# A two-layer mixed trunk on one core: turning products over four PSUM banks, partial sums kept in the rows, rope cut in two, weight and token sums placed one by one

## The chip, the cores and the metric

The kernel runs on one core of a Trainium2 chip. The metric is the device time of one launch in microseconds. The engines are named as in the profile: PE (TensorE matmul, with PEld for its weight loads), DVE (VectorE), ACT (ScalarE), POOL (GpSimd) and SP (SyncE, whose queue issues most transfers). All engines take their instructions in order; they meet at semaphores only.

## The reference: what is computed

A trunk of two layers over 512 tokens of width 1024, with 256 context tokens, all in fp32. The first layer (window attention beside a two-way state-space scan) is not touched. The second is a differential attention over the 768 tokens; cut to what matters:

```python
q, k, v, g = split(h @ w_in, 4)              # h: 768 x 1024 (q, g only for the 512 tokens), w_in: 1024 x 4096
q, k = rope(rms_norm(q, q_norm)), rope(rms_norm(k, k_norm))   # per 64-wide half head; context keys have no rope
s = einsum('bqhcd,bkhcd->bchqk', q, k) * 64 ** -0.5           # 8 heads, 2 components c
p = softmax(s)
o = einsum('bhqk,bkhv->bqhv', p[:, 0] - lam * p[:, 1], v)
o = rms_norm(o, head_norm) * (1 - lambda_init)
x = x + gate * ((o * silu(g)) @ w_out)
```

## The kernel before

The program is one list of stages, `STAGES`, written out by hand; every engine walks the same list and does its own part of each stage. The order of the list is therefore the order of work on PE, DVE, ACT and POOL alike. `stages_layer1` (line 265) writes the second layer.

**Products.** `h @ w_in` is done in eight slabs of 512 columns, in the order k1 0, q1 0, v1 0, g1 0, k1 1, q1 1, v1 1, g1 1. Within a slab two token tiles of 128 make a pair (three pairs with the context, two without), and a pair times a slab is done as a 2 x 2 block product with seven multiplications instead of eight, stages `("pr", kind, n, pair, i)` with i from 0 to 6. Each is four matmuls of depth 128 on 256 columns, which the trace shows as eight passes (line 1215). Products 0, 2, 4 and 6 add up in one PSUM bank, 1 and 3 in another (the cross bank), 5 stands alone. ACT copies 0, 1 and 2 out as partial sums and 6 as a final quarter (line 1979); DVE adds 3, 4 and 5 to the partial sums 2, 1 and 0 and so makes the other three quarters (line 1733). A product starts once the one before it in its bank has been copied or added out (`begin`, `unit_done`). Before the change `unit_banks` (line 368) gives products banks 0 and 1 alone, and the partial sums have three places of their own in the weight ring, so ACT waits for the add of the pair before (`PAIR_BEFORE`).

**Sums.** The block product needs sums of token blocks, four for a pair (`("sa", pair, j)`, lines 1753 to 1761), and sums of weight blocks, four for a slab (`("tw", slab, j)`, lines 1771 to 1781). All are DVE's. Products 1 to 4 of a pair wait for token sums 0 to 3; products 1, 2, 4 and 6 for weight sums 0 to 3.

**Rows of k1 and q1.** For each token tile: ACT squares the rows (line 1992), DVE reduces the squares by head (stage `heads`, line 1583), POOL makes the inverse root (lines 2148 and 2149), and DVE ropes the rows and multiplies by the root (stage `rope`; lines 1298, 1307 and 1309 inside `ropes`, and 1593). The first `heads` stage also makes the gain tables of the rope (lines 1314 and 1320) and sets `pads_ready` behind them (line 1573). ACT's copy of the very first product waits for that mark, because the rows of k1 lie over the raw rope table.

**Attention.** 32 steps (8 heads by 4 token tiles). In each: scores (PE, line 1243), their maxima (DVE, 1637), two exponentials (ACT, 2112), their difference (DVE, 1797), transposes of the step before (PE 1256, copied by ACT 2119), products with v (PE 1266), squares (ACT 2126) and the eviction times the gate (DVE 1806). The transposes of a step wait for line 1806 of an earlier one. Every fourth step ends with a head norm (root on POOL, DVE 1814). Stage `otr` transposes a finished head's output; DVE evicts the even heads (1820) and ACT the odd ones (2132). Some three to five products stand in each of the first 16 steps.

The place where such things stand in the list decides what waits for what. The first stages of the layer:

```python
st = [("k1", 0, 4), ("norm", 1, NX - 1), ("k1", 0, 5), ("tw", 0, 0), ("tw", 0, 1)]
st += [("trn", 1, k, 0) for k in range(KD)]
st += [("sa", 0, 0), ("sa", 0, 1), ("heads", "k1", 0, 4), ("sa", 0, 2), ("tw", 0, 2), ("sa", 0, 3),
       ("heads", "k1", 0, 5), ("tw", 0, 3)]
```

`trn` transposes the normed rows on PE; DVE (line 1397) and ACT (line 1900) evict them by turns into hT, which all products read.

## Time and profile before

| | us |
|---|---|
| median of 3 runs (lowest, highest) | 1134.08 (1131.03, 1134.19) |
| the profiled execution, its own time | 1134.98 |
| its span, first to last instruction | 1133.1 |
| PE busy | 1075.9 |
| DVE busy | 653.4 |
| ACT busy | 365.8 |
| POOL busy | 175.6 |

A row of a timeline gives the start and the length of one instruction or of several alike in a row, the engine, the line, the tiles out<-in, and in brackets how long the engine had stood idle before and what released it. The granted clock of PE is given as a share of 2.4 GHz. Durations of matmuls are modelled at their end, so the distance from start to start tells more than one row's length.

### The profile page before, as it was taken

To read this page: it belongs to the slowest core of one execution; us is meant where nothing else is said; L and a number is where in the kernel's file an instruction comes from. 1 tells how busy PE (TensorE), PEld (TensorE's weight loads), DVE (VectorE), ACT (ScalarE), POOL (GpSimd) and SP (SyncE) were. 2 spreads that over 40 slices of the span, in tenths; PEclk is the share of its full clock that TensorE was granted. 3 is DMA by queue.
4 is the path that set the end of the run, shared out by engine and by line. 5 is a ranking of instruction groups with operands and counts; after the bars stand their busy time and mean duration, and the time that the engine had idled before them with its cause. 6 is when DMAs were issued, how large, how long until landed. Compare 5 with 4: busy or idle time off the path is not lost. (4 is left out here: it accounts for less than half of the span.)

```text
span 1133.1 us, 13225 instructions
## 1 busy us (share of the span) xinstructions
PE 1075.9 (95%) x4708; PEld 681.9 (60%) x4708; DVE 653.4 (58%) x1332; ACT 365.8 (32%) x872; POOL 175.6 (15%) x168
## 2 busy tenths in 40 slices
PE   4999999999999999999999987999998989999998
PEld 2665656555454444555544456787887768776663
DVE  0356677596727377776411247834577764577683
ACT  1522212145322344554200121212443333354450
POOL 0111000397623100000000003310022110000000
PEclk9899999999999999999999999999999989999999
DMA  9912440586750110010021030222202030204002
GB/s 353 338 10 79 154 158 6 183 286 215 257 224 31 56 57 1 1 56 1 1 79 51 37 126 0 76 74 75 75 2 74 1 112 1 75 1 149 1 1 75
DMA packets 50982, 100.64 MB, mean 89 GB/s; under 512 B 4388, under 2 KB 6309, under 8 KB 50917
## 3 DMA queue, kind: packets, MB, share of 16 engines
q1 hardware_dynamic: 44997, 88.77, 22.4%
q10 hardware_dynamic: 5664, 10.84, 2.6%
q0 software_dynamic: 256, 0.18, 0.4%
q8 instruction: 39, 0.64, 0.2%
q14 instruction: 26, 0.21, 0.1%
HBM read 93.38 MB, written 6.40 MB: 88 GB/s over the span
## 5 line engine op out<-in xcount | busy, mean ns | idle before, releaser
L928 PE MATMUL ps<-hT,ring 128*128 128x512 f32 (+1 forms) x512 | 169.8, 486 | 1.2 <-ACT pool_mem L1926 0.7
L1215 PE MATMUL ps<-ring,hT 128*128 128x256 f32 x608 | 140.4, 385 | 13.3 <-DVE pool_mem L1733 12.0
L928 PEld LDWEIGHTS ps<-hT,ring 128*128 128x128 f32 x512 | 95.8, 190 | 66.3 <-issue 60.3
L1215 PEld LDWEIGHTS ps<-ring,hT 128*128 128x128 f32 x608 | 114.7, 192 | 32.1 <-issue 15.9
L1215 PE MATMUL ps<-ring,xs_all 128*128 128x256 f32 x432 | 100.4, 389 | 6.6 <-ACT pool_mem L1979 3.0
L1215 PEld LDWEIGHTS ps<-ring,xs_all 128*128 128x128 f32 x432 | 83.4, 195 | 20.5 <-issue 8.8
L2148 POOL TENSOR_SCALAR stat<-stat 128x1 f32<-128x1 f32 (+2 forms) x32 | 9.1, 284 | 545.0 <-ACT pool_mem L1879 209.1
L1116 PE MATMUL ps<-ring,hT 128*128 128x512 f32 x192 | 88.4, 594 | 0.1
L1188 PE MATMUL ps<-ring,hT 128*128 128x512 f32 x192 | 85.8, 592 | 0.0
L1637 DVE TENSOR_REDUCE stat<-ps 128x1 f32<-128x768 f32 x64 | 60.9, 952 | 9.9 <-PE ps L1243 9.8
L1413 DVE SCALAR_TENSOR_TENSOR pool_mem<-ps,halftap,pool_mem 128x254 f32<-128x254 f32 (+3 forms) x96 | 59.1, 616 | 3.4
L2112 ACT ACTIVATE xs_all<-ps,stat 128x768 f32<-128x768 f32 x64 | 57.4, 903 | 11.1 <-DVE stat L1638 10.5
L1188 PEld LDWEIGHTS ps<-ring,hT 128*128 128x128 f32 x192 | 35.5, 190 | 40.2 <-issue 40.2
L928 PE MATMUL ps<-ring,pool_mem 128*128 128x512 f32 x128 | 57.8, 595 | 1.1 <-ACT pool_mem L2132 0.8
L1723 DVE TENSOR_TENSOR pool_mem<-ps,pool_mem 128x512 f32<-128x512 f32 x12 | 8.3, 692 | 84.2 <-PE ps L1188 84.2
L928 PE MATMUL ps<-ring,hT 128*128 128x512 f32 x128 | 56.0, 593 | 0.0
L1266 PEld LDWEIGHTS ps<-y_all,pool_mem 128*128 128x128 f32 x384 | 48.9, 195 | 7.3 <-issue 5.0
L1116 PEld LDWEIGHTS ps<-ring,hT 128*128 128x128 f32 x192 | 33.7, 190 | 30.6 <-issue 30.6
L1266 PE MATMUL ps<-y_all,pool_mem 128*128 128x128 f32 x384 | 48.9, 278 | 0.0
L2052 ACT COPY pool_mem<-ps 128x256 f32<-128x256 f32 (+2 forms) x48 | 26.2, 546 | 59.7 <-PE ps L1157 59.7
L1188 PE MATMUL ps<-ring,pool_mem 128*128 128x512 f32 x96 | 43.8, 593 | 0.0
L1088 PE MATMUL ps<-pool_mem 128*128 128x512 f32 x80 | 40.1, 626 | 2.8 <-DVE stat L1549 2.8
(226 smaller groups left out, 1629.7 us busy)
## 6 DMA issues: line engine op xcount, KB each, us to landing
ring<-in_mod_w_dram SPq DMA_DIRECT2D x10, 2048.0 KB, 8.7
ring<-in_od_w_in_dram SPq DMA_DIRECT2D x8, 2048.0 KB, 8.2
ring<-in_ev_w_in_dram SPq DMA_DIRECT2D x7, 2048.0 KB, 9.5
pool_mem<-la_rows_dram SPq DMA_DIRECT2D x24, 512.0 KB, 7.6
ring<-in_ev_w_out_dram SPq DMA_DIRECT2D x4, 1536.0 KB, 6.6
ring<-in_od_w_out_dram SPq DMA_DIRECT2D x2, 2048.0 KB, 10.0
ring<-in_mod_w_dram ACTq DMA_DIRECT2D x1, 2048.0 KB, 9.2
xs_all<-in_x_dram SPq DMA_DIRECT2D x4, 512.0 KB, 12.9
```

The source lines that it names most:

```text
L928: mm = pe.matmul(bank[:, 0:width], lhs_of(k), rhs_of(k), start=(k == 0), stop=(k == count - 1))
L1088: pe.matmul(ps[:, (2, 4)[n % 2], :], lhs, rhs, start=True, stop=True).then_inc(st_ready, 1)
L1116: mm = pe.matmul(bank, hT[:, k, t * P:(t + 1) * P], w[:, k, :], start=(k == 0), stop=(k == KD - 1))
L1188: mm = pe.matmul(bank, src[:, t * P:(t + 1) * P], slab_ap(("out0", n, k // 6))[:, k % 6, :], start=(k == 0), stop=(k == KM - 1))
L1215: mm = pe.matmul(bank[:, 0:NSPLIT], left[:, k, :], right[:, k, :], start=(k == 0 and i in (0, 1, 5)), stop=(k == KSPLIT - 1), skip_group_c ...
L1266: mm = pe.matmul(bank[:, 2 * P:3 * P], probT1[:, j, :], v1v[:, j, h * P:(h + 1) * P], start=(j == 0), stop=(j == NT - 1))
L1413: ins_ = V.scalar_tensor_tensor(out=dst[:, lo:hi], in0=src[:, lo + j - 2:hi + j - 2], scalar=tap(j), in1=dst[:, lo:hi], op0=ALU.mult, op1= ...
L1637: link(V.tensor_reduce(rmax[:, r:r + 1], pair(n)[:, 0:TOK], AXX, ALU.max))
L1723: V.tensor_tensor(tmp, bank_of(stage), gate, ALU.mult).then_inc(done_sem(stage), 1)
L2052: A.copy(probT[:, 0:nb, i, :], pt_bank[:, 0:nb * P].rearrange("p (b t) -> p b t", b=nb)).then_inc(pt_done, 1)
L2112: A.activation(prob1[:, c, :], pair(n)[:, 0:TOK], ACT.Exp, bias=nmax[:, r:r + 1], scale=SCALE, accum_out=rsum[:, r:r + 1]).then_inc(prob1_ ...
L2148: link(G.tensor_scalar(dst, src, 1.0 / count, EPS, ALU.mult, ALU.add))
```

## The change

- Products whose pair ends ahead of attention take the least recently used of four banks that isn't held (banks 0, 1, 7 and 5 of PSUM); later ones have banks 0 and 1 as before. PE waits once for the last use of bank 5 ahead of the first scores, and once for that of bank 7 ahead of the first transposed probabilities.
- ACT copies a partial sum straight to the rows that it belongs to, and DVE adds onto it in place. The three places in the ring and ACT's wait for the pair before are gone.
- The rope is two stages: part 0 multiplies by cosine and sine, part 1 adds the two and multiplies by the root. Parts are put into the list one behind each product. Where a tile's `heads` stage would have ended a step of attention, it now follows the first product of the next one.
- The weight sums of the next slab come behind products 0, 3 and 5 of the last pair and product 1 of the next slab (before: 0, 2, 4, 6). In the first slab the sums of the second and third pair come one behind each product; the sums of the first pair and all weight sums of the first slab stand ahead of product 0, and the `heads` stages of the context tiles behind products 0 and 1.
- ACT evicts all eight transposed outputs.

```diff
 def slab_products(s):
+    sums = {}
+    if s + 1 < len(IN_SLABS):
+        sums = {0: ("tw", s + 1, 0), 3: ("tw", s + 1, 1), 5: ("tw", s + 1, 2)}
...
-            if last and s + 1 < len(IN_SLABS) and i % 2 == 0:
-                piece.append(("tw", s + 1, i // 2))
+            if last and i in sums:
+                piece.append(sums[i])
+            if p == 0 and i == 1 and s >= 1:
+                piece.append(("tw", s, 3))
...
+def new_heads(piece):
+    return [u[1:] for u in piece if u[0] == "post" and u[1] != "g1"]
...
-    st = [("k1", 0, 4), ("norm", 1, NX - 1), ("k1", 0, 5), ("tw", 0, 0), ("tw", 0, 1)]
+    st = [("k1", 0, 4), ("norm", 1, NX - 1), ("k1", 0, 5), ("tw", 0, 0)]
     st += [("trn", 1, k, 0) for k in range(KD)]
-    st += [("sa", 0, 0), ("sa", 0, 1), ("heads", "k1", 0, 4), ("sa", 0, 2), ("tw", 0, 2), ("sa", 0, 3),
-           ("heads", "k1", 0, 5), ("tw", 0, 3)]
-    st += [("sa", 1, j) for j in range(4)]
+    st += [("sa", 0, 0), ("sa", 0, 1), ("tw", 0, 1), ("sa", 0, 2), ("sa", 0, 3), ("tw", 0, 2), ("tw", 0, 3)]
+    extra = {(0, 0): ("heads", "k1", 0, 4), (0, 1): ("heads", "k1", 0, 5), (0, 2): ("rope", 1, "k1", 0, 4),
+             (0, 3): ("sa", 1, 0), (0, 4): ("sa", 1, 1), (0, 5): ("rope", 1, "k1", 0, 5), (0, 6): ("sa", 1, 2),
+             (0, 7): ("sa", 1, 3), (1, 0): ("sa", 2, 0), (1, 2): ("sa", 2, 1), (1, 4): ("sa", 2, 2), (1, 6): ("sa", 2, 3),
+             (2, 10): ("hk", 0, 1), (2, 13): ("hk", 0, 0), (2, 17): ("hq", 0)}
...
             st += piece
-            st += squares
-            squares = head_stages(piece, "heads")
-            if ropes and j % 7 in (0, 2):
+            st += [("heads",) + u for u in squares]
+            if ropes:
                 st.append(ropes.pop(0))
-            ropes += head_stages(piece, "rope")
+            ropes += [("rope", part) + u for u in fresh for part in range(2)]
+            fresh, squares = squares, new_heads(piece)
...
-            if j == min(1, len(now) - 1) and waiting:
-                st.append(waiting[0])
-            if j == 3 and two:
-                st.append(waiting[1])
-        st += squares
-        squares = []
+            if ropes and (j >= 1 or len(now) == 1):
+                st.append(ropes.pop(0))
+            ropes += [("rope", part) + u for u in fresh for part in range(u[2] >= NX, 2)]
+            fresh, squares = squares, new_heads(piece)
...
-BANKS = (0, 1, 7)
+BANKS = (0, 1, 7, 5)
...
-                bank[m] = min((b for b in range(2) if b not in held), key=lambda b: last[b])
+                free = [b for b in ((0, 1, 2, 3) if STAGES.index(u[:4] + (6,)) < attention else (0, 1)) if b not in held]
+                bank[m] = min(free, key=lambda b: last[b])
...
                         pe.wait_ge(prob_ready, len(SCORE))
+                        pe.wait_ge(unit_done[3], UNIT_BANK.count(3))
...
                         pe.wait_ge(pt_done, len(SCORE))
+                        pe.wait_ge(unit_done[2], UNIT_TURN[UNIT[PV1S[0]]])
...
-                        V.tensor_tensor(odd_rows(sub, n, t)[:, half * NSPLIT:(half + 1) * NSPLIT],
-                                        bank_of(stage)[:, 0:NSPLIT], part_sum[5 - i], ALU.add
+                        rows = product_rows(*a)
+                        V.tensor_tensor(rows, bank_of(stage)[:, 0:NSPLIT], rows, ALU.add
...
-                            dst = part_sum[i]
-                            if (sub, n, p) in PAIR_BEFORE:
-                                wait_done(act, ("pr",) + PAIR_BEFORE[(sub, n, p)] + (5 - i,))
                         if stage == ("pr", "k1", 0, 0, 0):
                             act.wait_ge(pads_ready, 2)
-                        A.copy(dst, bank_of(stage)[:, 0:NSPLIT]).then_inc(done_sem(stage), 1)
+                        A.copy(product_rows(*a), bank_of(stage)[:, 0:NSPLIT]).then_inc(done_sem(stage), 1)
...
-                    if h % 2 == 1:
-                        wait_unit(act, stage)
+                    wait_unit(act, stage)
+                    A.activation(oT[h], bank_of(stage), ACT.Copy, scale=head_gain).then_inc(done_sem(stage), 1)
```

## Rows read from the trace of the kernel before

**Rows 1.** The page's first part: busy us (share of span) and instructions of each engine.

```profile
PE 1075.9 (95%) x4708; PEld 681.9 (60%) x4708; DVE 653.4 (58%) x1332; ACT 365.8 (32%) x872; POOL 175.6 (15%) x168
```

**Rows 2.** Stretches of layer 2: from:to, length, busy PE, PEld, DVE, ACT, POOL, clock, DMA.

```profile
674.00:782.00 108.00, 96.49 (x437) 81.95 (x438) 66.34 (x132) 19.02 (x45) 25.69 (x20) 0.98 0.17 59
...
782.00:1024.00 242.00, 226.63 (x1222) 185.07 (x1223) 154.28 (x305) 95.15 (x218) 26.44 (x28) 0.98 0.12 43
...
680.00:720.00 40.00, 32.41 (x142) 27.44 (x141) 32.02 (x60) 5.87 (x13) 15.22 (x12) 0.96 0.15 53
```

**Rows 3.** Timeline, all engines, 670 to 690: start, length, engine, line, tiles, [idle before].

```profile
670.07 1.23 DVE L1777 TENSOR_TENSOR ring<-ring 128x1024 f32<-128x1024 f32 x1
...
672.16 1.94 PE L997 MATMUL ps<-consts,y_all 128*128 128x128 f32 x16 [1.72 <-DVE hT L1397]
...
675.07 0.69 DVE L1753 TENSOR_TENSOR xs_all<-hT 128x512 f32<-128x512 f32 x1 [0.48 <-ACT hT L1900]
...
675.08 1.97 PE L1215 MATMUL ps<-ring,hT 128*128 128x256 f32 x8 [0.97 <-DVE hT L1397]
...
676.40 0.42 DVE L1314 TENSOR_TENSOR pool_mem<-pool_mem,bc 128x256 f32<-128x256 f32 x1
...
678.27 0.15 DVE L1573 COPY stat<-ones 128x1 f32<-128x1 f32 x1
...
678.51 0.66 ACT L1979 COPY ring<-ps 128x256 f32<-128x256 f32 x2 [3.54 <-DVE stat L1573]
...
679.03 3.69 PE L1215 MATMUL ps<-ring,xs_all 128*128 128x256 f32 x16 [0.26 <-ACT ring L1979]
...
680.18 1.22 DVE L1779 TENSOR_TENSOR ring<-ring 128x1024 f32<-128x1024 f32 x1
...
689.65 6.79 PE L1215 MATMUL ps<-ring,hT 128*128 128x256 f32 x24 [5.20 <-DVE pool_mem L1733]
```

**Rows 4.** The same timeline, on DVE: one product's add, and one rope.

```profile
693.03 0.42 DVE L1733 TENSOR_TENSOR pool_mem<-ps,ring 128x256 f32<-128x256 f32 x1 [3.19 <-PE ps L1215]
...
696.53 0.68 DVE L1298 TENSOR_TENSOR pool_mem<-pool_mem 128x512 f32<-128x512 f32 x1
...
698.06 0.69 DVE L1309 TENSOR_TENSOR pool_mem<-pool_mem 128x512 f32<-128x512 f32 x1
...
698.78 0.69 DVE L1593 TENSOR_TENSOR pool_mem<-pool_mem,dcd 128x512 f32<-128x512 f32 x1
```

**Rows 5.** Timeline of PE alone, 690 to 790.

```profile
696.28 5.34 PE L1215 MATMUL ps<-ring,xs_all 128*128 128x256 f32 x24
...
704.50 5.42 PE L1215 MATMUL ps<-ring,hT 128*128 128x256 f32 x24 [1.15 <-DVE pool_mem L1733]
...
755.26 0.41 PE L945 MATMUL ps<-consts,pool_mem 128*128 128x128 f32 x2 [0.61 <-DVE y_all L1733]
```

**Rows 6.** Timeline, all engines, 842 to 882.

```profile
856.52 1.97 PE L1215 MATMUL ps<-ring,pool_mem 128*128 128x256 f32 x8 [2.22 <-ACT ring L1979]
...
862.10 2.77 PE L1215 MATMUL ps<-ring,hT 128*128 128x256 f32 x8 [1.89 <-DVE pool_mem L1733]
...
867.42 0.69 DVE L1583 TENSOR_REDUCE dcd<-pool_mem 128x8 f32<-128x512 f32 x1 [0.81 <-ACT pool_mem L1992]
...
868.48 0.88 PE L1256 MATMUL ps<-consts,xs_all 128*128 128x128 f32 x6
```

**Rows 7.** Timeline, all engines, 896 to 932.

```profile
906.75 0.69 DVE L1583 TENSOR_REDUCE dcd<-pool_mem 128x8 f32<-128x512 f32 x1 [0.81 <-ACT pool_mem L1992]
...
910.85 0.69 DVE L1814 TENSOR_TENSOR pool_mem<-pool_mem,stat 128x512 f32<-128x512 f32 x1 [3.16 <-POOL stat L2149]
...
915.12 8.39 PE L1215 MATMUL ps<-ring,xs_all 128*128 128x256 f32 x24 [3.03 <-ACT pool_mem L1979]
```

**Rows 8.** Timeline, all engines, 946 to 984.

```profile
976.85 0.80 ACT L2119 COPY pool_mem<-ps 128x768 f32<-128x768 f32 x1 [2.27 <-PE ps L1256]
...
978.60 5.42 PE L1215 MATMUL ps<-ring,xs_all 128*128 128x256 f32 x24 [1.79 <-DVE pool_mem L1820]
```

More of the change, by code:

```diff
@@ L257, in slab_products @@
     return out
-def head_stages(piece, name):
-    return [(name,) + u[1:] for u in piece if u[0] in ("post", "k1") and u[1] != "g1"]
+def new_heads(piece):
+    return [u[1:] for u in piece if u[0] == "post" and u[1] != "g1"]
 def stages_layer1():
-    st = [("k1", 0, 4), ("norm", 1, NX - 1), ("k1", 0, 5), ("tw", 0, 0), ("tw", 0, 1)]
+    st = [("k1", 0, 4), ("norm", 1, NX - 1), ("k1", 0, 5), ("tw", 0, 0)]
     st += [("trn", 1, k, 0) for k in range(KD)]
-    st += [("sa", 0, 0), ("sa", 0, 1), ("heads", "k1", 0, 4), ("sa", 0, 2), ("tw", 0, 2), ("sa", 0, 3),
-           ("heads", "k1", 0, 5), ("tw", 0, 3)]
-    st += [("sa", 1, j) for j in range(4)]
-    turns = {10: ("hk", 0, 1), 13: ("hk", 0, 0), 17: ("hq", 0)}
-    squares, ropes = [], [("rope", "k1", 0, 4), ("rope", "k1", 0, 5)]
+    st += [("sa", 0, 0), ("sa", 0, 1), ("tw", 0, 1), ("sa", 0, 2), ("sa", 0, 3), ("tw", 0, 2), ("tw", 0, 3)]
+    extra = {(0, 0): ("heads", "k1", 0, 4), (0, 1): ("heads", "k1", 0, 5), (0, 2): ("rope", 1, "k1", 0, 4),
[3 rows of a table added]
+    squares, ropes, fresh = [], [], []
     for s in range(3):
@@ L275, in stages_layer1 @@
             st += piece
-            st += squares
-            squares = head_stages(piece, "heads")
-            if ropes and j % 7 in (0, 2):
+            st += [("heads",) + u for u in squares]
+            if ropes:
                 st.append(ropes.pop(0))
-            ropes += head_stages(piece, "rope")
-            if s == 1 and j in (0, 2, 4, 6):
-                st.append(("sa", 2, j // 2))
-            if s == 2 and j in turns:
-                st.append(turns[j])
-    assert not ropes and not squares
+            ropes += [("rope", part) + u for u in fresh for part in range(2)]
+            fresh, squares = squares, new_heads(piece)
+            if (s, j) in extra:
+                st.append(extra[(s, j)])
+    assert not ropes and not squares and not fresh
     fill = [piece for s in range(3, len(IN_SLABS)) for piece in slab_products(s)]
@@ L307, in stages_layer1 @@
         now = [fill.pop(0) for _ in range(STEP_PRODUCTS[n])] if n < len(STEP_PRODUCTS) else [outs.pop(0)]
-        waiting = ropes
-        two = len(waiting) > 1 and len(now) > 3
-        ropes = waiting[1 + two:]
         for j, piece in enumerate(now):
             st += piece
-            st += squares
-            squares = head_stages(piece, "heads")
-            ropes = ropes + head_stages(piece, "rope")
+            st += [("heads",) + u for u in squares]
             if j == 0:
                 st.append(("comb1", h, t))
-            if j == min(1, len(now) - 1) and waiting:
-                st.append(waiting[0])
-            if j == 3 and two:
-                st.append(waiting[1])
-        st += squares
-        squares = []
+            if ropes and (j >= 1 or len(now) == 1):
+                st.append(ropes.pop(0))
+            ropes += [("rope", part) + u for u in fresh for part in range(u[2] >= NX, 2)]
+            fresh, squares = squares, new_heads(piece)
         if n >= 1:
@@ L330, in stages_layer1 @@
             st.append(("hnorm", n // 4 - 1))
-    assert not fill and not ropes
+    assert not fill and not ropes and not fresh and not squares
     st += [("ptr1",) + work[-1]] + outs.pop(0) + [("pv1",) + work[-1], ("hnorm", C_HEADS - 1)]
@@ L370, in unit_banks @@
     bank, turn = [None] * len(UNITS), [None] * len(UNITS)
-    last, turns, held, sums, cross = [-2, -1, -3], [0, 0, 0], set(), None, None
+    last, turns, held, sums, cross = [-2, -1, -3, -4], [0, 0, 0, 0], set(), None, None
+    attention = STAGES.index(("sc1", 0, 0, 0))
     for n, s in enumerate(STAGES):
@@ L1288, in _, with ropes @@
             V = nc.vector
-            def ropes(src, groups, wtab, wrow, token_tile, ta, tb):
+            def ropes(src, groups, wtab, wrow, token_tile, ta, tb, part=None):
                 v = src.rearrange("p (h d) -> p h d", d=HD)
@@ L1295, in ropes @@
                     link(V.tensor_tensor(a, v, wrow.unsqueeze(1).to_broadcast([P, groups, HD]), ALU.mult))
+                    return
+                if part == 1:
+                    link(V.tensor_tensor(ta[:, 0:groups * HD], ta[:, 0:groups * HD], tb[:, 0:groups * HD], ALU.add))
                     return
```

29 lines of the change are left out of this document (11 added, 18 removed).

## Prediction

> **What bounds the kernel now.** I read the page's busy shares first, then the stretches of the second layer, then PE's waits there in order of time. PE is busy for 1075.9 us of the span [rows 1], and the chain that ends last runs on PE, so only PE's gaps and its slow stretches can be won. The diff touches the second layer from its first product on. There PE stands still for 11.5 of the 108 us up to the first attention score, and for 15.4 of the 242 us in which products and attention are mixed (span less busy time) [rows 2]. The clock matters as well: a stretch of three products takes 5.34 us at full clock [rows 5], 6.79 us after the long gap in the first pair [rows 3] (the granted clock of 680 to 720 is 0.96 of 2.4 GHz on the mean [rows 2], so a part ran at 1.2 GHz) and 8.39 us after a later gap [rows 7]. So a gap can be paid twice, once as idle time and once at the lower of the two clock levels. I price every edit by what PE waited for at that place, and take its clock loss from the row behind the gap.
>
> One product is eight passes; three take 5.34 us with an overlap of 0.15 us, so one is worth about 1.73 us [rows 5].
>
> **The change, part by part.**
>
> *Start of the layer.* Before, the second weight sum (1.23 us) runs on DVE ahead of its evictions of the normed rows, and PE then waits 1.72 us for such an eviction [rows 3]. The change puts that sum behind the evictions. The wait shrinks to about 0.4 us and everything up to the first product comes 1.3 us earlier: product 0 at 673.8 instead of 675.1.
>
> *A new wait, at the third product.* ACT may copy product 0 only when the raw rope table has been read, since the rows of k1 lie over it. Before, DVE made four sums short of that: two token sums, then the gain tables from 676.40, done with the marker at 678.27; ACT copied at 678.51 and PE's third product started at 679.03 with 0.26 us of waiting [rows 3]. In the changed order all four token sums and three weight sums stand on DVE ahead of the gain tables: 4 x 0.7 + 3 x 1.2 = 6.4 us, from 673.8 to 680.2; the tables take 2.0 us (676.40 to the end of the marker at 678.42), so the marker falls at 682.2 and the third product starts 0.6 us later, at 682.8. Products 0 and 1 end at 677.3. That is a gap of 5.5 us on PE, and on ACT the copies of products 0 and 1 queue behind it. The third product adds into the bank of product 0, so four banks don't help.
>
> *The old gap goes.* Before, product 5 waited 5.20 us, to 689.65, because DVE had weight sums, the next pair's token sums and two ropes ahead of one add [rows 3]. Now these sums are spread one behind each add. Products 2, 3 and 4 run behind the new gap; with the slow clock of the old one (6.65 us net for three, from 6.79) product 5 starts at 682.8 + 6.65 = 689.4. The next pair starts two products later, at 692.9; before it was 689.65 + 6.79 - 1.73 = 694.7. Gain 1.8 us. Bounds: 3.2 us if the clock stays up (5.34 instead of 6.79), 0.2 us if it falls as in the 8.39 us row.
>
> *Four banks, and rope in two stages, in the k1 and q1 slabs.* In the three following pairs product 5 waits for the add of product 3, 1.15 to 1.24 us each, three rows of which one stands [rows 5]: with two banks it needs that bank, and DVE does a whole rope first (2.9 us, 696.53 to the end of 698.78 [rows 4]). With four banks product 5 takes another bank, and the waiting one is product 6, which needs the add of product 4. Behind the add of product 3 (0.42 us) DVE has a weight sum (1.2), the first rope stage (1.5 us: 696.53 to 698.06) and then the add of product 4: 3.6 us, against two products, 3.46 us. I leave 0.3 us of waiting in two of the three pairs: gain 3.0 us; between 0 (DVE falls behind, it is busy for 32.02 of 40 us there [rows 2]) and 3.6. The ropes' second stages hold only adds that nobody waits for so soon.
>
> *The three transposes of heads ahead of attention.* Two of them wait 0.61 us for an add (one row stands [rows 5]). In the new turn they fall on banks 0 and 1 when these hold nothing fresh. Gain 1.2 us (0 to 1.2). PE's two added waits at the first scores and the first transposed probabilities stand ahead of everything on PE, but the last products in those banks are four products old; nothing, or at most 0.61 us if the cover is gone.
>
> *Partial sums in the rows.* The same copies and adds, the same sizes; only ACT's wait for the pair before goes, and no PE gap rests on it. Nothing.
>
> *Attention, step with both ropes and a head norm ahead (850 to 868).* PE's gap of 2.22 us comes from ACT copying late behind its exponentials and stays [rows 6]. The 1.89 us at 862.10 goes: the add now comes behind one rope stage. But DVE must still do two weight sums, two ropes, three adds before it evicts the attention output that the next transposes wait for (868.48), and the only thing that leaves the step is one squares reduction with its wait for ACT (0.81 + 0.69 us, of which some is given back in hand-overs): that transpose comes 0.7 us earlier, and the gap moves ahead of it, now some 3 us in one piece. If the clock answers as behind the other gap of this size (3.03 us, then 8.39 instead of 5.34 [rows 7]), up to 3.05 us are lost where before the slow stretch was hidden. I take half, 1.6: a loss of 0.9 us, between a gain of 0.7 and a loss of 2.4.
>
> *Attention, step 896 to 915.* Here the same reduction (0.81 of wait, 0.69 of work) moves across the step's end, and with it POOL's root. In the old order POOL makes that root first and the head norm's root behind it, so DVE stands 3.16 us at 910.85, the scores' maxima and the exponentials come late, ACT copies late, and PE waits 3.03 us at 915.12 and then runs slowly [rows 7]. In the new order the head norm's root is long made. DVE reaches the norm when its step's work is done, 0.8 us before the old reduction's end at 907.4 plus 0.35 us for the eviction, about 907.05; 3.8 us earlier, and the products with it. No gap of that length is left ahead of them, so I also count the clock: 8.39 - 5.34 = 3.05. Gain 6.9 us (3.8 to 6.9).
>
> *Transposed outputs evicted by ACT alone.* At 978.60 PE waits 1.79 us for DVE's eviction behind two maxima [rows 8]. ACT stands idle for 2.27 us at that point, ahead of its copy at 976.85. Its own eviction of 512 columns takes no more than that copy of 768, 0.80 us. Gain 1.65 us (0 to 1.8). The other three turns hang on nothing; the last costs ACT at most 0.1 us on the final chain.
>
> **Sum.** 1.8 + 3.0 + 1.2 - 0.9 + 6.9 + 1.65 - 0.1 = 13.55 us. The profiled execution took 1134.98 us (span 1133.1), so 1121.4; the median of the runs is 0.9 us lower, and on that footing 1120.5.
>
> A rule speaks against the first half. The Trainium skill, "TensorE: Matmul & The Clock Gate", section "HAM oscillation — how this bites in real kernels", reports a kernel in which double-buffering in PSUM brought no further gain. By it the 3.0 and 1.2 us would not come and the time would be 1124.7. The trace so far speaks for a gain, since those gaps end on an add and not on data, but DVE's load leaves the rule room.
>
> **Rivals.**
> 1. *The gaps only move: DVE is the bound.* Four banks put off the moment at which DVE is late, by one product, and its work is the same. For it: 32.02 of 40 us busy [rows 2]. Against it: in the q1 slab DVE has time, and PE waits little over 1 us per pair. Then only the start (0.2 to 1.8), the transposes, the output eviction and the lower end of the 915 step come: 0.2 + 1.2 + 1.65 + 3.8 - 2.4 = 4.5 to 6; 1128 to 1129.6.
> 2. *The clock falls in the products: slower.* If the quicker turn of four banks leaves PE many short gaps and the clock goes down through the 49 products, each product costs more. At the pace of the 8.39 us row one costs 2.75 instead of 1.73 us; over 49 that is 50 us, over half of them 25. It decides from 14 slow products on, where the 13.55 us are eaten up; with 25 the time is about 1146. Against it: in the old order gaps of 1.15 us recur each 13 us at full pace (5.42 for three products [rows 5]). The Trainium skill, same page, section "A second HAM failure mode: psum-queue depth-cycling", describes such a kernel; no row here shows it.
> 3. *The change does not do what it says.* The new wait on the rope table is followed by the slow clock at its worst, the banks are blocked by the in-order DVE, and the 915 step hangs on something else (ACT's exponentials). Left are the start's 0.2, the transposes' 0 to 1.2 and the eviction's 0 to 1.65, so 0.2 to 3 us: 1131 to 1134.
>
> **How the numbers follow.** Forecast 0.62, with its own range from the bounds 1117 to 1128; rival 1 0.22; rival 3 0.11; rival 2 0.05. A measurement of this kernel can tell about 0.3% (3.4 us) from no change. Faster: forecast and rival 1 and a little of rival 3, 0.86; same 0.09; slower 0.05. The range runs from 1116 (clock kept everywhere) to 1129 (rival 1's middle).
>
> **What would show it.** Right: a PE gap near 5.5 us ahead of the third product, ended by ACT's copy behind the marker; no gap ahead of product 5 in k1 and q1; first scores some 6 us earlier; no wait of DVE for POOL at the head norm near 905; no 1.79 us gap behind the third head's output. Wrong: the gap at the third product missing or twice as long, product 6 waiting a microsecond or more per pair, or a granted clock below full in the q1 and v1 slabs.

## The result, and the profile after

| | before | after |
|---|---|---|
| median of 4 runs each (lowest, highest), us | 1132.77 (1131.03, 1134.19) | 1115.39 (1113.58, 1116.42) |
| ratio, 95% interval | | 0.9846 [0.9823, 0.9868] |
| the profiled execution and its span, us | 1134.98, 1133.1 | 1113.58, 1111.5 |
| first product of layer 2 to the first of the last 32 passes of the output, us | 440.85 | 422.93 |

The change saves 17.4 us by the medians. The direction came; the gain was put at 13.55 us, so the time lies 1.6 us under the forecast's own range (1117 to 1128) and 0.6 us under the whole one (1116 to 1129).

The page's busy parts of the changed kernel, to be read against [rows 1]:

```profile
PE 1070.2 (96%) x4708; PEld 680.6 (61%) x4708; DVE 650.3 (59%) x1328; ACT 368.1 (33%) x876; POOL 173.7 (16%) x168
```

PE's 4708 matmuls are the same. DVE lost four instructions and ACT has four more: the even heads' outputs. Busy times barely move; it is PE's idle time that moved. Stretches of the changed kernel's second layer (from:to, length, busy PE, PEld, DVE, ACT, POOL, clock, DMA):

```profile
674.00:770.00 96.00, 90.72 (x415) 78.64 (x415) 63.74 (x128) 17.41 (x42) 22.48 (x20) 0.98 0.17 58
770.00:1002.00 232.00, 224.28 (x1227) 184.18 (x1226) 151.86 (x303) 96.81 (x220) 27.46 (x28) 0.99 0.14 48
674.00:690.00 16.00, 11.13 (x44) 9.16 (x44) 11.57 (x28) 1.65 (x4) 4.00 (x4) 0.89 0.00 0
690.00:720.00 30.00, 29.75 (x139) 25.89 (x138) 28.44 (x58) 7.02 (x16) 12.79 (x12) 1.00 0.20 71
```

Ahead of the first scores PE now stands for 5.3 us, before for 11.5; in the mixed stretch for 7.7, before for 15.4 [rows 2]. Nearly all that is left of the first lies in one place, 674 to 690, where the granted clock is 0.89. Behind it, from 690 to 720, PE is busy for 29.75 of 30 us at full clock, beside a DVE that is busy for 28.44.

The timeline of PE in the changed kernel, from the transposes of the normed rows to the third pair (start, length, line, tiles, [idle before]):

```profile
668.47 1.94 PE L998 MATMUL ps<-consts,y_all 128*128 128x128 f32 x16 [0.46 <-DVE hT L1405]
671.38 1.97 PE L1216 MATMUL ps<-ring,hT 128*128 128x256 f32 x8 [0.97 <-DVE hT L1405]
673.18 1.89 PE L1216 MATMUL ps<-ring,xs_all 128*128 128x256 f32 x8
679.94 5.38 PE L1216 MATMUL ps<-ring,xs_all 128*128 128x256 f32 x16 [4.87 <-ACT pool_mem L1977]
685.16 7.07 PE L1216 MATMUL ps<-ring,hT 128*128 128x256 f32 x32
692.07 5.34 PE L1216 MATMUL ps<-ring,xs_all 128*128 128x256 f32 x24
697.25 3.62 PE L1216 MATMUL ps<-ring,hT 128*128 128x256 f32 x16
701.12 3.69 PE L1216 MATMUL ps<-ring,hT 128*128 128x256 f32 x16 [0.25 <-DVE pool_mem L1744]
...
725.68 3.69 PE L1216 MATMUL ps<-ring,hT 128*128 128x256 f32 x16 [0.15 <-DVE pool_mem L1744]
...
746.48 0.38 PE L946 MATMUL ps<-consts,pool_mem 128*128 128x128 f32 x2
```

Against [rows 3]: the wait of 1.72 us is 0.46, the gap of 5.20 us ahead of product 5 is gone, and a new one of 4.87 us stands ahead of the third product, ended by ACT's copy. Against [rows 5]: the three waits of 1.15 to 1.24 us are two of 0.25 and 0.15, and the transposes of heads wait for nothing.

The same timeline in the two steps of attention, and at the third head's output:

```profile
846.03 2.57 PE L1216 MATMUL ps<-ring,pool_mem 128*128 128x256 f32 x8 [2.01 <-ACT pool_mem L1977]
848.39 4.74 PE L1216 MATMUL ps<-ring,hT 128*128 128x256 f32 x16
...
856.60 0.85 PE L1259 MATMUL ps<-consts,xs_all 128*128 128x128 f32 x6 [0.63 <-issue]
...
894.44 0.85 PE L1259 MATMUL ps<-consts,xs_all 128*128 128x128 f32 x6 [1.13 <-issue]
...
898.62 5.42 PE L1216 MATMUL ps<-ring,xs_all 128*128 128x256 f32 x24
...
957.01 5.42 PE L1216 MATMUL ps<-ring,xs_all 128*128 128x256 f32 x24 [0.21 <-ACT pool_mem L2129]
```

And DVE there: the mark on the rope table, the norm of the first head, the eviction that the transposes at 856.60 wait for, and the norm of the second head:

```profile
679.19 0.15 DVE L1581 COPY stat<-ones 128x1 f32<-128x1 f32 x1
...
841.80 0.69 DVE L1824 TENSOR_TENSOR pool_mem<-pool_mem,stat 128x512 f32<-128x512 f32 x1 [3.15 <-POOL stat L2145]
...
856.15 0.34 DVE L1816 SCALAR_TENSOR_TENSOR pool_mem<-ps,stat,pool_mem 128x128 f32<-128x128 f32 x1
...
894.25 0.68 DVE L1824 TENSOR_TENSOR pool_mem<-pool_mem,stat 128x512 f32<-128x512 f32 x1
```

Against [rows 7]: the second head's norm at 894.25 no longer waits 3.16 us for POOL, and the three products at 898.62 follow without a gap and at full clock, 5.42 instead of 8.39 us. The first head's norm still waits 3.15 us (3.64 before), and PE still stands for 2.01 us at 846.03; of the two gaps of [rows 6], the second (1.89) is gone.

**Where the 21.6 us between the two spans lie.** 2.44 us lie in front of the second layer, in code that the change doesn't touch: the first product starts at 675.08 [rows 3] and at 671.38, 3.70 earlier, of which the shorter wait explains 1.26. The same code reached its first product anywhere from 670.38 to 674.93 in the experiments that leave this stretch alone (4 and 8 are these two), so this is how executions differ by themselves. That leaves 19.2 us, which the table takes apart by the starts of like rows; three fifths of it are attention's.

| part | forecast | by the rows |
|---|---|---|
| to the second pair's first product (with the 1.26) | 1.8 | 1.8 |
| waits inside the three pairs | 3.0 | 3.2 |
| waits of the heads' transposes | 1.2 | 1.2 |
| the rest up to the first scores | not in the sum | 1.4 |
| from the first scores to the end of the gap at 856.52, with a wait of 0.41 us of the transposes ahead of [rows 6] | not in the sum | 0.46 |
| from the gap at 856.52 to the transposes at 868.48 [rows 6] | -0.9 | 1.4 |
| on to the end of the slow products at 915.12 [rows 7] | 6.9 | 7.6 |
| on to the third head's output [rows 8] | 1.65 | 2.1 |
| behind it, with the final chain | -0.1 | 0.0 |

### The profile page after: what moved, and what is told of

It reads as the page before. It is cut to its first block and busy times, and to the rows that moved or that the text cites. A ratio compares the mean times of both kernels' runs of the same rounds, so it can differ in the third digit from the quotient of the medians.

```text
span 1111.5 us, 13171 instructions
## 1 busy us (share of the span) xinstructions
PE 1070.2 (96%) x4708; PEld 680.6 (61%) x4708; DVE 650.3 (59%) x1328; ACT 368.1 (33%) x876; POOL 173.7 (16%) x168
## 5 line engine op out<-in xcount | busy, mean ns | idle before, releaser
L1216 PE MATMUL ps<-ring,hT 128*128 128x256 f32 x608 | 137.6, 382 | 1.5 <-DVE hT L1405 1.0
L1216 PEld LDWEIGHTS ps<-ring,hT 128*128 128x128 f32 x608 | 114.9, 192 | 17.9 <-issue 1.5
L1189 PEld LDWEIGHTS ps<-ring,hT 128*128 128x128 f32 x192 | 35.5, 190 | 40.2 <-issue 40.2
L1117 PEld LDWEIGHTS ps<-ring,hT 128*128 128x128 f32 x192 | 33.7, 190 | 31.0 <-issue 31.0
L929 PEld LDWEIGHTS ps<-ring,hT 128*128 128x128 f32 x128 | 24.0, 190 | 28.7 <-issue 28.7
```

What stands on the lines that cost most here:

```text
L929: mm = pe.matmul(bank[:, 0:width], lhs_of(k), rhs_of(k), start=(k == 0), stop=(k == count - 1))
L1117: mm = pe.matmul(bank, hT[:, k, t * P:(t + 1) * P], w[:, k, :], start=(k == 0), stop=(k == KD - 1))
L1189: mm = pe.matmul(bank, src[:, t * P:(t + 1) * P], slab_ap(("out0", n, k // 6))[:, k % 6, :], start=(k == 0), stop=(k == KM - 1))
L1216: mm = pe.matmul(bank[:, 0:NSPLIT], left[:, k, :], right[:, k, :], start=(k == 0 and i in (0, 1, 5)), stop=(k == KSPLIT - 1), skip_group_c ...
```

## The experiments

All start from the changed kernel. Ratios are to the kernel before. Medians of two kernels that lie less than some 2 us apart don't settle anything by themselves; there the rows do, and the layer's length as in the last line of the first table (422.93 us in the changed kernel).

**1. Products in two banks.** One line makes the four banks two again (with the one wait that belongs to the fourth); the order of the work stays.

```diff
-                free = [b for b in ((0, 1, 2, 3) if STAGES.index(u[:4] + (6,)) < attention else (0, 1)) if b not in held]
+                free = [b for b in (0, 1) if b not in held]
```

> The changed kernel with products in banks 0 and 1 only, all else as changed. If the banks carry their two terms (3.0 us for products, 1.2 us for transposes of heads), the time rises by 3 to 4.4 us over the changed kernel and PE waits about 1.2 us ahead of product 5 in three pairs. Rival: the order of DVE's work carries the first term. In the trace of the changed kernel the add of product 3 runs 0.2 us after that product ends (697.45 after 697.25), so two banks would not make product 5 wait; then only the transposes' waits come back, 0.6 us each: 1 to 1.5 us slower.

Measured: 1116.85 us, 0.9855 [0.9829, 0.988]; the layer 424.61 us. No wait came back ahead of product 5 in any pair, and product 6 waits 0.26 and 0.15 us as in the changed kernel. What came back are the transposes' waits (timeline of PE in this kernel; the first row is product 6 of the second pair, the last two are its step of attention):

```profile
703.08 3.69 PE L1216 MATMUL ps<-ring,hT 128*128 128x256 f32 x16 [0.26 <-DVE pool_mem L1743]
...
749.21 0.41 PE L946 MATMUL ps<-consts,pool_mem 128*128 128x128 f32 x2 [0.61 <-DVE y_all L1743]
...
763.17 0.63 PE L946 MATMUL ps<-consts,pool_mem 128*128 128x128 f32 x4 [0.61 <-DVE y_all L1743]
...
850.01 1.97 PE L1216 MATMUL ps<-ring,pool_mem 128*128 128x256 f32 x8 [2.02 <-ACT pool_mem L1976]
...
860.46 0.84 PE L1258 MATMUL ps<-consts,xs_all 128*128 128x128 f32 x6 [2.20 <-issue]
```

From the last three products ahead of the first transposes to the first scores this kernel takes 32.55 us (743.26 to 775.81), the changed one 30.54 (741.30 to 771.84): 2.0 us, of which 1.2 are the two waits and 0.8 hand-overs that the timeline doesn't mark as waits. So the four banks are worth 2.0 us by the rows, all around these transposes, and 1.5 by the medians; they are not worth the 3.0 us of the pairs. The Trainium skill, "TensorE: Matmul & The Clock Gate", section "HAM oscillation — how this bites in real kernels", reports a kernel in which double-buffering in PSUM gave no further gain. Here two more banks gave 2.0 us by the rows, little but not nothing; the 3.0 us came all the same, by the order of DVE's work.

**2. The `heads` stage back to the end of its step of attention.**

```diff
             fresh, squares = squares, new_heads(piece)
+        st += [("heads",) + u for u in squares]
+        fresh, squares = fresh + squares, []
```

> The changed kernel, but a squares reduction whose rows are ready at the end of a step of attention stays at that step's end (with POOL's root of it), as it stood before the change. If the order of the two roots on POOL makes the gap at 915 of the kernel before, DVE again stands about 3 us for POOL at the head norm of the step near 894, products behind it start 3.8 us later and the clock falls: 4.5 to 7.5 us slower. Rival: that gap went with the earlier end of DVE's work (rope in two stages); then 0 to 1 us slower, and DVE's wait for POOL stays under 1 us.

Measured: 1121.56 us, 0.9896 [0.9866, 0.9927]; 6.2 us slower than the changed kernel, the layer 8.1 longer. The edit also moves the rope parts of these rows up by one product. POOL, DVE and PE, one timeline each:

```profile
897.59 1.64 POOL L2147 TENSOR_TENSOR dcd<-dcd,stat 128x8 f32<-128x8 f32 x1
899.31 0.20 POOL L2146 TENSOR_SCALAR stat<-stat 128x4 f32<-128x4 f32 x1
899.59 1.01 POOL L2147 TENSOR_TENSOR stat<-stat 128x4 f32<-128x4 f32 x1
```

```profile
900.63 0.69 DVE L1826 TENSOR_TENSOR pool_mem<-pool_mem,stat 128x512 f32<-128x512 f32 x1 [3.16 <-POOL stat L2147]
```

```profile
857.46 0.84 PE L1261 MATMUL ps<-consts,xs_all 128*128 128x128 f32 x6 [2.79 <-issue]
858.14 5.31 PE L1218 MATMUL ps<-ring,hT 128*128 128x256 f32 x16
...
904.91 7.11 PE L1218 MATMUL ps<-ring,xs_all 128*128 128x256 f32 x24 [3.03 <-ACT pool_mem L1979]
```

The chain at 897 to 905 is read off from POOL to PE: POOL makes the rows' root of 128 x 8 first and the head's root of 128 x 4 behind it; DVE's norm starts where the second ends, after 3.16 us; ACT copies late; PE stands for 3.03 us and then runs three products in 7.11 us. The waits of 3.16 and 3.03 us have the lengths of [rows 7]. From the transposes at 857.46 to the end of the slow products it takes 7.1 us more than in the changed kernel: 3.7 for the later start of these three products, 1.7 for their clock (7.11 instead of 5.42), and 1.7 for the clock of the two products at 858.14 (5.31 instead of 3.62), which the kernel before did not lose there. This is the mechanism of the largest term of the sum, and it is shown: one reduction that moves past the end of a step takes POOL's root out of the norm's way.

**3. The rope in one piece.** Both stages stand back to back where the first one stood.

```diff
-                st.append(ropes.pop(0))
-            ropes += [("rope", part) + u for u in fresh for part in range(2)]
+                st += ropes.pop(0)
+            ropes += [both for u in fresh for both in ([("rope", part) + u for part in range(2)], [])]
```

> The changed kernel with both rope stages back to back at the place of the first. If the two stages matter for PE: in the k1 and q1 slabs the add of product 4 stands behind a weight sum and a whole rope (2.9 instead of 1.5 us), product 6 waits about 1.5 us in two pairs (0.25 and 0.15 now), 2.6 us together; in attention the add of product 3 comes 1.4 us later in two steps, 0.5 us each: 2.5 to 4.5 us slower. Rival: the placement of sums and the four banks take all up, the rope's cut brings nothing: within 1 us.

Measured: 1119.93 us, 0.9881 [0.9855, 0.9906]; 4.5 us slower, the layer 4.7 longer. The timeline of DVE between the adds of products 3 and 4 of one pair, and of PE:

```profile
699.11 0.42 DVE L1746 TENSOR_TENSOR pool_mem<-ps,pool_mem 128x256 f32<-128x256 f32 x1 [0.50 <-PE ps L1218]
699.55 1.23 DVE L1789 TENSOR_TENSOR ring<-ring 128x1024 f32<-128x1024 f32 x1
...
703.55 0.75 DVE L1746 TENSOR_TENSOR pool_mem<-ps,pool_mem 128x256 f32<-128x256 f32 x2
```

```profile
704.11 2.18 PE L1218 MATMUL ps<-ring,hT 128*128 128x256 f32 x9 [1.58 <-DVE pool_mem L1746]
```

From one add to the next DVE needs 4.44 us, PE for its two products 3.46; product 6 waits for the difference and what the adds themselves take, with four banks free or not. The waits at product 6 in the slabs ahead of attention are 1.58, 0.35, 1.48 and 0.35 us, 3.4 more than in the changed kernel. With experiment 1 this settles what the 3.0 us are: the order of DVE's work between two adds.

**4. The even heads' outputs evicted by DVE.** DVE gets its stage back, ACT keeps the odd heads.

```diff
+                elif kind == "otr":
+                    h = a[0]
+                    if h % 2 == 0:
+                        wait_unit(dve, stage)
+                        V.tensor_scalar(oT[h], bank_of(stage), head_gain, None, ALU.mult
+                                        ).then_inc(done_sem(stage), 1)
```

> The changed kernel with the even heads' transposed outputs evicted by DVE again. If the 1.79 us gap went with the eviction's engine, it comes back behind the third head (0.21 us now) and nowhere else: 1.6 us slower, to 2.1. Rival: DVE reaches that eviction early enough in the new order; then no gap and no change.

Measured: 1115.71 us, 0.9849 [0.9818, 0.9879]: by the medians no difference. The timeline of PE, its first product of the layer and the third head's output:

```profile
670.38 1.97 PE L1216 MATMUL ps<-ring,hT 128*128 128x256 f32 x8 [0.97 <-DVE hT L1405]
...
958.65 5.42 PE L1216 MATMUL ps<-ring,xs_all 128*128 128x256 f32 x24 [1.79 <-DVE pool_mem L1830]
```

The wait of [rows 8] is back to the hundredth, against 0.21 us in the changed kernel: 1.58 us at this place. So the term of 1.65 stands by the row. The medians don't show that it reaches the end, but the rows do: from the first scores to the last 32 passes this kernel takes 324.27 us, the changed one 322.47, and the kernels of experiments 1 and 5 to 8, which keep ACT's eviction and the order of attention, 322.37 to 322.39.

**5. The second weight sum ahead of the evictions again.**

```diff
-    st = [("k1", 0, 4), ("norm", 1, NX - 1), ("k1", 0, 5), ("tw", 0, 0)]
+    st = [("k1", 0, 4), ("norm", 1, NX - 1), ("k1", 0, 5), ("tw", 0, 0), ("tw", 0, 1)]
```

(`("tw", 0, 1)` leaves its place among the token sums.)

> The changed kernel with the second weight sum of the first slab ahead of the transposes again. By the term in the prediction the first product comes 1.3 us later and the time rises by 1.3 us. Rival: the gap ahead of the third product is set by the length of DVE's chain (four token sums, three weight sums, gain tables), which is as long either way; then the first product comes 1.2 us later, the gap shrinks from 4.9 to 3.7 us, and the time doesn't change.

Measured: 1114.60 us, 0.984 [0.9814, 0.9867]. PE's timeline:

```profile
673.29 1.94 PE L998 MATMUL ps<-consts,y_all 128*128 128x128 f32 x16 [1.72 <-DVE hT L1405]
...
683.76 6.52 PE L1216 MATMUL ps<-ring,xs_all 128*128 128x256 f32 x16 [3.86 <-ACT pool_mem L1977]
```

The wait of 1.72 us is back, and the gap is 3.86 instead of 4.87 us: what the first product loses, the third gets back, all but 0.25 us. DVE has the same list to work through up to the mark. The 1.3 us at the head of the layer are no gain of their own, as the rival had it; the first two products only run earlier towards the same third one.

**6. The gain tables and their mark behind the second weight sum.** They become a stage of their own, ahead of two token sums and two weight sums.

```diff
-    st += [("sa", 0, 0), ("sa", 0, 1), ("tw", 0, 1), ("sa", 0, 2), ("sa", 0, 3), ("tw", 0, 2), ("tw", 0, 3)]
+    st += [("sa", 0, 0), ("sa", 0, 1), ("tw", 0, 1), ("tables",), ("sa", 0, 2), ("sa", 0, 3), ("tw", 0, 2), ("tw", 0, 3)]
```

> The changed kernel with the gain tables and their mark moved up, behind the second weight sum; the sums that followed it follow the tables. If the mark sets the gap ahead of the third product (4.9 us, then 5.4 us for two products instead of 3.6), it shrinks to about 1.5 us and the clock stays up; DVE then has the adds late and product 6 waits about 1.3 us: 2 to 4 us faster. Rival: the gap is DVE's whole load and only moves to product 6: within 1 us.

Measured: 1111.58 us, 0.9803 [0.9782, 0.9824]; 3.8 us faster, the layer 3.8 shorter:

```profile
678.15 3.69 PE L1216 MATMUL ps<-ring,xs_all 128*128 128x256 f32 x16 [1.40 <-DVE xs_all L1769]
...
686.51 3.69 PE L1216 MATMUL ps<-ring,hT 128*128 128x256 f32 x16 [1.21 <-DVE pool_mem L1744]
```

The third product waits 1.40 us, now for a token sum, and runs at full pace; product 6 waits 1.21 us for an add.

**7. The raw rope table in a place of its own.** The rows of k1 don't lie over it any more, and ACT's wait for the mark moves to the first product of q1, whose rows do.

```diff
-        rope_raw1 = carve(0, 512).rearrange("p (a t d) -> p a t d", a=2, t=NX)
+        rope_raw1 = carve(6144, 512).rearrange("p (a t d) -> p a t d", a=2, t=NX)
...
-                        if stage == ("pr", "k1", 0, 0, 0):
+                        if stage == ("pr", "q1", 0, 0, 0):
```

> The changed kernel with the raw rope table in a place that q1's rows take later, and the wait for the mark at q1's first product: no wait for the mark at k1. DVE's order is as changed. If the mark makes the gap but DVE is nearly full there, the gap ahead of the third product goes and about 3 us of it come back ahead of product 6, which waits for the add of product 4 behind tables, two reductions and a rope: 2 to 3.5 us faster. Rival (DVE has room): the whole 4.9 and 1.8 us go: 5 to 6.6 us faster.

Measured: 1110.10 us, 0.9794 [0.9773, 0.9814]; 5.3 us faster, the layer 3.8 shorter. Products 0 to 5 run without a gap, and then product 6 waits:

```profile
684.98 3.69 PE L1216 MATMUL ps<-ring,hT 128*128 128x256 f32 x16 [2.85 <-DVE pool_mem L1744]
```

Experiments 6 and 7 show the new wait as the forecast had it: the mark behind all sums of the first pair. They also show what stands behind it. Without any wait for the mark 2.85 of the 4.87 us come back at product 6, for the add of product 4, which DVE reaches late, as expected; the 1.8 us of slow clock (5.38 instead of 3.62) don't, and so the gain is above the 2 to 3.5 us expected. At these places of the first slab DVE has more to do than PE's products cover.

**8. Partial sums in the ring again**, with ACT's wait for the pair before.

```diff
-                        V.tensor_tensor(rows, bank_of(stage)[:, 0:NSPLIT], rows, ALU.add
+                        V.tensor_tensor(rows, bank_of(stage)[:, 0:NSPLIT], part_sum[5 - i], ALU.add
```

> The changed kernel with the partial sums in three places of their own again and ACT's wait for the add of the pair before. If that part is worth nothing, as the prediction has it: within 0.5 us. Rival: ACT's wait now binds, since the next pair's first three copies stand behind adds that the spread-out sums delay; then ACT copies late and PE waits some tenths per pair, 1 to 3 us slower.

Measured: 1115.80 us, 0.984 [0.9815, 0.9865]; the layer 423.97 us. No wait that the changed kernel lacks appears on PE. The 1.0 us more of the layer are the clock's, behind the same gap:

```profile
683.50 6.50 PE L1220 MATMUL ps<-ring,xs_all 128*128 128x256 f32 x16 [4.88 <-ACT ring L1983]
```

This part of the change is worth nothing that the rows or the medians show, as put.

**9. The head's norm ahead.** In the steps that end with a norm it moves up, behind the first product of its step. On POOL the head's root then stands ahead of the two roots of rows, on DVE the norm well ahead of the maxima.

```diff
                 st.append(("comb1", h, t))
+                if n >= 5 and n % 4 == 1:
+                    st.append(("hnorm", n // 4 - 1))
...
-        if n >= 5 and n % 4 == 1:
-            st.append(("hnorm", n // 4 - 1))
```

> The changed kernel with each head norm behind the first product of its step, so that POOL makes its root ahead of the roots of that step's rows. If the gap of 2.0 us near 846 comes from POOL making the head norm's root third, behind two others (DVE stands 3.15 us at 841.80), it goes, and the slow clock behind it too (2.57 and 4.74 us where full pace is 1.9 and 3.6): 2 to 3.7 us faster. Rival: the exponentials come no earlier, since DVE reaches the maxima at the same time: within 0.5 us.

Measured: 1112.21 us, 0.9824 [0.9806, 0.9843]; 3.2 us faster, the layer 2.0 shorter. POOL makes the head's root (128 x 4) first, DVE's norm finds it done, and the gap of 2.01 us at 846.03 is gone. So that gap, which the prediction put down to ACT's exponentials and took as given, also began with the order of roots on POOL. What is left in this step is the wait of the transposes. POOL, DVE and PE, one timeline each:

```profile
828.92 1.01 POOL L2145 TENSOR_TENSOR stat<-stat 128x4 f32<-128x4 f32 x1
...
836.84 2.08 POOL L2145 TENSOR_TENSOR dcd<-dcd,stat 128x8 f32<-128x8 f32 x1
```

```profile
834.82 0.68 DVE L1824 TENSOR_TENSOR pool_mem<-pool_mem,stat 128x512 f32<-128x512 f32 x1
```

```profile
844.03 1.89 PE L1216 MATMUL ps<-ring,pool_mem 128*128 128x256 f32 x8
...
853.92 0.85 PE L1259 MATMUL ps<-consts,xs_all 128*128 128x128 f32 x6 [1.72 <-issue]
```

**10. DVE's work in the first slab thinned out.** With the table apart as in 7, the tables and the first reduction of the context tiles go behind product 4, the second reduction behind product 5, and ropes and token sums that nobody needs at once go into the next two slabs, where DVE has time. (The third pair's token sums stood in the second slab, q1, and not in the first as the list of the change has it; they go into the third.)

```diff
-    extra = {(0, 0): ("heads", "k1", 0, 4), (0, 1): ("heads", "k1", 0, 5), (0, 2): ("rope", 1, "k1", 0, 4),
...
+    extra = {(0, 3): [("sa", 1, 0)], (0, 4): [("heads", "k1", 0, 4)], (0, 5): [("heads", "k1", 0, 5), ("sa", 1, 1)],
...
+    slots = {(1, j) for j in (0, 2, 3, 4, 6, 8, 9, 11)} | {(2, j) for j in (0, 2, 4, 6, 7, 8, 9, 11)}
...
-            if ropes:
+            if (s, j) in slots:
```

> The changed kernel with the raw rope table in a place of its own, and DVE's work of the first slab thinned out: tables and context reductions behind product 4, ropes of k1 in the q1 slab, ropes of q1 and the third pair's token sums in the v1 slab. If the start's loss is the mark and then DVE's load, both gaps go: no gap over 1 us from the first product to the first scores, 5 to 6.6 us faster. Rival: ropes that come later make the heads' transposes or the adds late, and 3 us or more of waits come back in the q1 and v1 slabs: 1 to 3 us faster.

Measured: 1107.99 us, 0.9779 [0.976, 0.9799]; 7.4 us faster than the changed kernel, the layer 7.0 shorter, more than the 5 to 6.6 us expected. Up to the first scores it is 7.7 us shorter; 0.7 are lost again behind them, at the gap that experiment 9 removes (below). The stretch from just behind the first product to the first scores in this kernel (columns as above):

```profile
674.00:766.00 92.00, 92.00 (x432) 80.44 (x432) 65.36 (x130) 17.99 (x43) 22.91 (x20) 1.00 0.20 69
```

PE is busy for 92.00 of 92 us at full clock. DVE is busy for 65.36 us of it: it was never the bound of the slabs as a whole, only of places in them.

**11. Experiments 9 and 10 together.**

> Both of the two edits before. If they act at different places, their gains add up: 7 to 10 us faster than the changed kernel, near 1107. Rival: what one gains the other's stretch gives back, less than the sum of both by over 2 us.

Measured: 1104.59 us (1102.57 to 1105.63), 0.9746 [0.9724, 0.9769]; the layer 413.41 us, 9.5 shorter than in the changed kernel (7.0 + 2.0 for the two alone): 7.7 up to the first scores, as in experiment 10, and 1.8 behind them, as in experiment 9. It is 10.8 us faster than the changed kernel and 28 faster than the kernel before.

## Why the forecast was right in direction and 4 us short

Two steps of the prediction failed. Its mechanism for the three pairs, "With four banks product 5 takes another bank", did not bring their gain. And most of the missing time lies in the step from 850 to 868, put at -0.9 us and measured at 1.4, and in what the sum left out, 1.9 us. The parts in turn:

**The start: right in size, its parts only in the sum.** The gap ahead of the third product was put at 5.5 us and is 4.87: the mark ended at 679.34, 8.0 us behind the first product's start, where 8.4 were reckoned. The two products behind it took 5.38 us instead of 3.62, as the forecast's use of the slow row had it. The 1.3 us at the head were counted into this term only through their sum, and experiment 5 shows that this was needed: alone they are worth nothing.

**The three pairs: right size, wrong cause.** 3.0 was put, 3.2 came. The step that failed is "With four banks product 5 takes another bank": by experiment 1 product 5 doesn't wait with two banks either, since DVE adds product 3 in time once no whole rope stands ahead of it, and by experiment 3 product 6 waits for DVE with four. The size came because the prediction also counted DVE's list between two adds with the rope cut (3.6 us against 3.46), and left 0.3 us in two pairs; 0.25 and 0.15 came. Rival 1's mechanism (DVE's order decides, not the banks) thus holds in these slabs, yet its time doesn't: the cut of the rope was part of the change, and DVE's list then fits beside two products.

**The transposes of heads** are the place where the banks count: 1.2 us of waits, as put, and 0.8 us of hand-overs beside them that were not in the sum (experiment 1).

**Partial sums in the rows:** nothing, as put (experiment 8).

**The step from 850 to 868: the wrong sign.** -0.9 was put, 1.4 came, the largest piece of what is missing. Two terms failed. Of the reduction that leaves the step, with its wait (0.81 + 0.69), only 0.7 us were counted and the rest written off to hand-overs; DVE's chain from the head norm to the eviction that the transposes wait for became shorter by nearly all of it, from 15.75 us in the kernel before (DVE's timeline there, below) to 14.35 (841.80 to 856.15).

```profile
852.28 0.69 DVE L1814 TENSOR_TENSOR pool_mem<-pool_mem,stat 128x512 f32<-128x512 f32 x1 [3.64 <-POOL stat L2149]
...
868.03 0.34 DVE L1806 SCALAR_TENSOR_TENSOR pool_mem<-ps,stat,pool_mem 128x128 f32<-128x128 f32 x1
```

And the clock loss of 1.6 us, taken at half from another gap, didn't come. The gap ahead of the transposes did not grow to the 3 us of the forecast: it is 0.63 us, and the two products behind it ran at full pace (3.62 us). The slow stretch stood ahead of it instead. In the changed kernel the products behind the gap of 2.01 us ran slowly (2.57 and 4.74 us), and the transposes, waiting for DVE's eviction at 856.15, then stood for 0.63 us; from product to transposes 10.57 us. In experiment 1 the same products ran at full pace behind 2.02 us (1.97) and the transposes stood for 2.20 us; 10.45 us. So the slow clock used up time in which PE would have waited. This is no rule, though: experiment 10 has the same gap, a slower product behind it, and a loss (timeline of this kernel, PE and DVE):

```profile
839.34 3.21 PE L1218 MATMUL ps<-ring,pool_mem 128*128 128x256 f32 x8 [2.01 <-ACT pool_mem L1979]
842.64 0.42 DVE L1746 TENSOR_TENSOR pool_mem<-ps,pool_mem 128x256 f32<-128x256 f32 x1 [0.79 <-DVE pool_mem L1315]
...
850.55 0.85 PE L1261 MATMUL ps<-consts,xs_all 128*128 128x128 f32 x6 [1.27 <-issue]
```

DVE's add starts 0.09 us behind the slow product's end, after 0.79 us of waiting (0.16 in the changed kernel, also 0.09 behind the product's end), and the transposes come 11.21 us behind the product, 0.76 later than in experiment 1, although PE still stands for 1.27 us. A slow stretch ahead of a wait that DVE ends is free only as far as DVE does not wait for one of the slow products on its way there. And the loss that the forecast feared does come when the gap ahead of the transposes is longer: in experiment 2 it was 2.79 us, and two products behind it took 5.31 us.

**The step from 896 to 915:** 6.9 was put, 7.6 came, of which 3.0 are the three products' clock (8.39 to 5.42 us), as put. The other 4.6 are the 46.64 us from the transposes at 868.48 to the products at 915.12 [rows 6, 7], now 42.02 from 856.60 to 898.62, where 3.8 were put. Experiment 2 shows the mechanism and gives back 3.7 of the 4.6. The other 0.9 stay open; the rope's cut is not their cause, since experiment 3, with the rope whole, takes 42.01 us over the same stretch (862.57 to 904.58).

**The outputs' eviction:** 1.65 put, 1.58 of it by the wait (experiment 4); the other 0.5 us of that row of the table lie in two rows of four products, at 927.42 and 965.42, which took 7.38 and 7.32 us before where the changed kernel takes 7.07; their cause no run here takes apart.

**What was not in the sum.** 1.4 us up to the first scores: hand-overs that the timeline doesn't mark as waits. 0.8 of them stand around the transposes of heads and hang on the banks (experiment 1); the other 0.6 lie in two pairs further ahead and stay open. And 0.46 us between the first scores and the end of the gap at 856.52, where a wait of the transposes was left out. Together 1.9; with 2.3 of the step from 850 to 868, 0.7 and 0.5 of the two behind it, and 0.3 in the three pairs and the last line of the table, that makes some 5.7 us by the rows, 19.2 less 13.55; by the medians the forecast was short by 3.8. The two executions shown are not the median ones: they lie 2.2 us above theirs before and 1.8 below theirs after, and 2.44 of these 4.0 us stand in front of the layer. Up to 1.1 us of the rest may be a clock event: two products behind the long gap took 5.38 us in the execution shown, and 6.50 and 6.52 us in those of experiments 8 and 5. What they took in the other executions of the changed kernel no run here shows.

**The rivals.** The clock didn't fall in the products (1.00 from 690 to 720), but for the two behind the gap. The Trainium skill's section "A second HAM failure mode: psum-queue depth-cycling" (page as above) describes a kernel whose clock moves to and fro as it turns over banks; four banks did not do this here. That the change doesn't do what it says is out by experiments 2 and 3.

## What to carry to other kernels

Ask of a wait for a buffer who empties it and what else stands in that engine's list between two such evictions: here the cut of one 2.9 us piece on DVE was worth 4.7 us of layer time (experiment 3), two more banks 1.7 (experiment 1). Before a shared unit with a queue, such as the engine that makes roots, the short request that a chain waits for must not stand behind one that can wait. And a mark that guards a buffer belongs right behind the buffer's last use, ahead of work that can wait, or the buffer needs a place of its own: that wait, with what hid behind it on DVE, cost 7.7 us up to the first scores (experiment 10), as much as the change had won there (7.6).

## What the chip showed beyond expectation

The clock behind a gap is no fixed price. Gaps of 3.86 to 4.88 us ahead of the third product, in the changed kernel and seven of the experiments (1 to 5, 8 and 9), were followed by slow products each time: two took 5.15 to 6.52 us instead of 3.62. Behind 2.79 us in experiment 2 two took 5.31; behind 2.85 and 2.20 us in experiments 7 and 1 they ran at full pace. The gap of 2.0 to 2.2 us at 846.03 (856.52 in the kernel before) was followed by a slow product in three kernels (2.57 us in the changed one, 3.58 and 3.21 in experiments 3 and 10) and by one at full pace, 1.97 us, in the kernel before and in experiments 1, 2 and 4 to 8. For gaps of this size a forecast can only take both ends.

By the profile, POOL's root of 128 x 8 elements took 1.64 us and that of 128 x 4 took 1.01 (experiment 2; the one in experiment 9's rows took 2.08). Ahead of each stands a step of 0.20 us that scales its argument. So of DVE's 3.16 us about 1.3 are the head's own root and the rest is the root that stood in front of it; half the elements save only 0.63 us.
